# A layer norm moved in between the last output blocks, with its scale and shift folded into the next input

## The chip, the core and the metric

One core of a Trainium2 chip runs the whole program in one launch. The metric is the time of one execution in microseconds on the device, as the median of several runs. The engines are PE (matrix products, with PEld loading its stationary operand), DVE (vector), ACT (activation functions), POOL (GpSimd) and SP, which only issues DMAs here. PSUM is the memory that PE writes, SBUF the one that all engines work in, DRAM what lies behind the DMAs.

## The reference

Four layers on `x` of 512 tokens by 1024 channels, in float32: two of a block that runs an HGRN2 and an RWKV7 mixer side by side, then one RG-LRU and one retention layer with RMS norms. What matters here is how a layer of the first block begins and ends:

```
cond = silu(c) @ w_ada[l] + b_ada[l]
shift, scale, gate_raw = split(cond, 3)
h = x * (1.0 + scale) + shift
proj = h @ w_in[l]
...
out = merged @ w_out[l]
x = layer_norm(DN_ALPHA * x + (1.0 + gate_raw) * out, ln_g[l], ln_b[l])
```

`layer_norm` takes the mean and the variance over the 1024 channels of a token, multiplies by rsqrt(var + 1e-5), then by `g`, and adds `b`. After layer 1 the RG-LRU layer begins with `rms_norm(x, pre0)`, whose sum of squares runs over the same channels.

## The kernel before

Activations are held transposed: channels on the 128 partitions, the 512 tokens along the free axis, so that `x` is eight tiles `xa[:, m, :]` of 128x512. All weights pass through one stream of blocks of eight 128x128 tiles. SP loads block b into one of two buffers `w_raw` (L559), ACT rounds it into `w_hi` (`weights(b)`, L778), POOL writes the rest into `w_lo` (`low`, L702). Activations are split in the same way: ACT writes `act_hi` (`high`, L786), DVE `act_lo` (`low`, L1253). A product is three matmuls, hi·hi, hi·lo and lo·hi; `project` (L1910) does one block of 24 into one of two PSUM banks, `side_by_side` (L1930) four output tiles at once into four banks, taking the input tiles one after the other.

All five engines run programs of their own, in the written order, and meet at counting semaphores. `weights(b)` waits until PE has used block b-2, and SP loads a block when POOL has done with the one two before it. Every engine's order is fixed by hand; there is no planner.

A layer ends so. `side_by_side` makes output tiles 0 to 3, four blocks `b_out+4` to `b_out+7` make tiles 4 to 7. For each tile DVE adds gate times output onto `xa` (`out_added`, L1256). PE sums the channels with a product by a matrix of ones, in plain float32, which is two records in the trace for each tile (`add_up`, L2308): tiles 0 to 3 behind block `b_out+4`, then each tile behind the block after its own. Then, in this order: DVE subtracts the mean from eight tiles; ACT squares each into one of two buffers `ST` (L793) and PE sums the squares (L1952), by turns; ACT makes rsqrt as Ln and Exp (L798, L800), each behind a load of its function table; DVE multiplies each tile by it (L1253) and applies `ln_g`, `ln_b` (L1698), by turns over the eight tiles.

The next layer begins with `modulated` (L1331): DVE writes `x * (1 + scale) + shift` into `ST`, ACT and DVE split it, and PE starts `side_by_side(("rw", l))` on the first tile. ACT's order there is `high` for tiles 0 to 3, `weights(b_rw+2)`, `high` for 4 and 5, `weights(b_rw+3)`, `high` for 6 and 7, `weights(b_rw+4)`, `weights(b_rw+5)`. `x` itself is needed again at the end of the layer, and SP stores it in DRAM:

```
blocks_to(b_rw + 4)
if l:
    sp.wait_ge(S("x_done"), KT * l)
    sp.dma_start(x_scr[0].rearrange("k p t -> p k t"), xa[:, :, :]).then_inc(S("x_saved"), 16)
    blocks_to(b_rw + 6)
    sp.wait_ge(S("x_saved"), 16)
```

`blocks_to(n)` issues the loads of all blocks below n, so the load of block `b_rw+4` stands behind the wait for eight `x_done`. After layer 1 the RMS norm squares `xa` in the same way and PE sums the squares before the first product of the RG-LRU layer. `Chain.done` makes an engine wait for its own instruction.

Of the kernel before, what the change touches and what calls it, by code (L numbers as in the profile page):

```python
# [15 lines left out]
ALU = mybir.AluOpType  # L16
# [4 lines left out]
D = 1024  # L21
# [174 lines left out]
def job_plan():  # L196
    jobs = Jobs()
    for l in range(DEPTH):
# [102 lines left out]
            jobs.add(("out", l, i), i, signalled=False)  # L301
        jobs.add(("ln_mean", l), 4)
        jobs.add(("ln_var", l), 5)
    jobs.add("rms_pre0", 4)
    for i in range(4):
        jobs.add(("lru_in", 0, i), i, signalled=False)
# [47 lines left out]
def build(nc, shapes):  # L354
# [10 lines left out]
    with ExitStack() as ctx:  # L365
# [32 lines left out]
        for name, n in [("c", 8), ("lb_t", 12), ("cl", RT), ("cl_t", RT)] + [  # L398
                (f"{k}{l}", n) for l in range(DEPTH)
                for k, n in (("mu1", 17), ("omlb", 4), ("lbf", 4), ("ka1", 4))]:  # L400
            derived_at[name] = derived[:, used:used + n]
            derived_first[name] = used
            used += n
# [55 lines left out]
        def evacuated(eng, b):  # L459

            u = use_of(b)
            eng.wait_ge(proj_read[u % 2], u // 2 + 2)

        def job_open(eng, name, turn=0):

            bank, use = jobs(name, turn)
            wait(eng, aux_read[bank], use)
            return aux[bank][:, :]

        def job_full(ins, name):  # L470
            return ins.then_inc(aux_full[jobs(name)[0]], 1)
# [295 lines left out]
        def _(act):  # L767
# [20 lines left out]
            def square(key, m, src):  # L788


                if m > 1:
                    act.wait_ge(sq_used, SQUARES[key] - list(SQUARES).index(key) + m - 1)
                A(ST[m % 2], src, ACT.Square).then_inc(sq_ready, 1)  # L793
# [286 lines left out]


            def squares(key, tiles, which, ready):
# [165 lines left out]
        def _(dve):  # L1248
# [3 lines left out]
            def tt(out_ap, a, b, op):  # L1252
                return TT(out_ap, a, b, op)  # L1253
# [60 lines left out]
            def conditioned(l, half, spans):  # L1314

                x = job_ready(dve, ("ada", l, half))
                for at, n in spans:
                    ins = tt(cond[:, l, at:at + n], x[:, at:at + n], V(f"b_ada{l}", at, n), ALU.add)
                    job_read(ins, ("ada", l, half)) if at == spans[-1][0] else ins
                evacuated_job(dve, ("ada", l, half))  # L1320
                for at, n in spans[1:]:
                    chain.done(TS(cond[:, l, at:at + n], cond[:, l, at:at + n], 1.0, None, ALU.add))

            def modulated(l, m):

# [35 lines left out]
            for l in range(DEPTH):  # L1361
# [2 lines left out]

                if l == 0:
                    conditioned(0, 1, ((4, 4), (12, 4)))
                tiles_of_h = range(KT) if l else range(4, KT)
                for m in tiles_of_h:
                    modulated(l, m)
                    if m > tiles_of_h[0]:  # L1370
                        low(SPLITS["h", l] + m - 1, m - 1, ST[(m - 1) % 2])
                low(SPLITS["h", l] + 7, 7, ST[1])
                if l == 0:
                    for n in range(LATER_AT[1]):
                        later_step(n)

# [59 lines left out]
                        .then_inc(S("rk_ready"), 1)  # L1436
                if l == 0:
                    conditioned(1, 0, ((0, 8), (8, 16)))
                for j in range(QT):
                    x = job_ready(dve, ("kk_sum", l, j))  # L1440
                    job_read(TS(xa[:, 4 + j, :], x, 1e-24, None, ALU.max), ("kk_sum", l, j))
# [237 lines left out]
                    else:  # L1679
                        read(ins, b_out + m)  # L1680

                for m in range(KT):
                    out_added(m)
                x = job_ready(dve, ("ln_mean", l))
                for m in range(KT):
                    if m < 4:
                        evacuated_job(dve, ("out", l, m))
                    else:
                        evacuated(dve, b_out + m)
                    ins = stt(xa[:, m, :], x, -1.0 / D, xa[:, m, :], ALU.mult, ALU.add)  # L1690
                    job_read(ins, ("ln_mean", l)) if m == 7 else ins.then_inc(S("xc_ready"), 1)
                dve.wait_ge(S("ln_rs"), l + 1)
                for m in range(KT + 1):
                    if m < KT:
                        tt(xa[:, m, :], xa[:, m, :], merged[:, 0, :], ALU.mult).then_inc(S("ln_scaled"), 1)
                    if m:
                        dve.wait_ge(S("ln_scaled"), KT * l + m)
                        TS(xa[:, m - 1, :], xa[:, m - 1, :], V(f"ln_g{l}", m - 1), V(f"ln_b{l}", m - 1),  # L1698
                           ALU.mult, ALU.add).then_inc(S("x_done"), 1)
                dve.wait_ge(S("x_done"), KT * (l + 1))  # L1700

            def normed(n, pre, count):

# [186 lines left out]
        def _(pe):  # L1890
# [44 lines left out]
            def used(ins):  # L1935

                ins.then_inc(block_used, 1)
# [18 lines left out]
            for l in range(DEPTH):  # L1956
# [344 lines left out]
                x = job_open(pe, ("ln_mean", l))  # L2301

                def add_up(m):
                    if m < 4:
                        evacuated_job(pe, ("out", l, m))
                    else:
                        evacuated(pe, b_out + m)
                    return MM(x, C("ones"), xa[:, m, :], start=(m == 0), stop=(m == 7))  # L2308

                for m in range(4, KT):  # L2310
                    used(project(b_out + m, tiles=(4, 5, 6, 7, 0, 1, 2, 3)))
                    for k in (range(4) if m == 4 else (m - 1,)):
                        add_up(k)
                job_full(add_up(7), ("ln_mean", l))
                sum_squares(("ln", l), ("ln_var", l))


            sum_squares("pre0", "rms_pre0")
# [181 lines left out]
```

## Time and profile before

| | |
|---|---|
| median of 3 runs | 2173.45 us (2170.6 to 2173.84) |
| profiled execution | 2173.69 us |
| its span | 2171.9 us |
| PE busy in the span | 1917.3 us (88%) |
| DVE, ACT, POOL busy | 1011.8, 865.7, 601.4 us |
| mean granted clock of PE | 0.956 |

Times in the profile count from the start of its span. A row of the timeline has the start, the length and, in brackets, how long the engine had been idle before it and what released it; "x8" behind it merges eight instructions. A PE matmul overlaps its neighbours, so that its pace is the distance of starts and not its length. A granted clock of 1.00 is 2.4 GHz, 0.50 is 1.2 GHz.

### The profile page before, as it was taken

The numbers are of one execution on the slowest core, as the hardware profiler recorded it, in microseconds if no ns is written. First come the engines' busy times: TensorE is split into PE (matmuls) and PEld (weight loads), VectorE is DVE, ScalarE is ACT, GpSimd is POOL, SyncE is SP. The second block draws the span as 40 slices with busy tenths as digits, with TensorE's granted clock in tenths as the row PEclk, the third lists the DMA queues.
The fourth block names the chain that finished last, engine by engine and source line by source line (L and its number), as shares of the span: only waits on it lengthen the run. The fifth ranks groups of instructions, "written<-read, shape, count | busy, mean of one in ns | idle before, by whom it ended". The sixth has DMA issues, their size and how long they took to land.

```text
span 2171.9 us, 35369 instructions
## 1 busy us (share of the span) xinstructions
PE 1917.3 (88%) x14368; PEld 1530.4 (70%) x14368; DVE 1011.8 (47%) x1327; ACT 865.7 (40%) x1236; POOL 601.4 (28%) x255
## 2 busy tenths in 40 slices
PE   4999988899997996988899998799687999998987
PEld 3777877699775684877798765666565886777755
DVE  7576376632535046375632635847605224132232
ACT  2333455533523333456433524256524332233332
POOL 1343432300242343422300331321232441322312
PEclk9899999999998898999999998899899999999999
DMA  8662222200423121222200423211133221211111
GB/s 325 215 223 68 80 90 82 68 4 4 171 91 111 62 95 58 88 82 72 69 4 18 170 87 145 78 59 39 43 117 112 97 97 39 78 55 62 59 66 71
DMA packets 60826, 192.89 MB, mean 89 GB/s; under 512 B 5632, under 2 KB 5888, under 8 KB 60320
## 3 DMA queue, kind: packets, MB, share of 16 engines
q1 hardware_dynamic: 60704, 191.10, 25.5%
q8 instruction: 97, 1.59, 0.3%
q14 instruction: 25, 0.20, 0.0%
HBM read 173.25 MB, written 17.83 MB: 88 GB/s over the span
## 4 chain that ended last, share of the span: by engine, by line
issue 57%; PE 24%; POOL 11%; DVE 4%; ACT 3%; POOLq 0%; DVEq 0%; ACTq 0%
PE proj L1910 13%; POOL w_lo_sb L702 10%; PE aux L2120 3%; PE aux L2051 2%; DVE area_sb L1253 2%; PE aux L2177 1%; PE proj L2120 1%; PE aux L2174 1%; ACT L798 1%; DVE area_sb L1256 0%; ACT L905 0%; PE aux L2107 0%; PE aux L1952 0%; PE aux L1941 0%; PE aux L2029 0%
## 5 line engine op out<-in xcount | busy, mean ns | idle before, releaser
L702 POOL TENSOR_TENSOR w_lo_sb<-w_raw_sb,w_hi_sb 128x1024 fp32r<-128x1024 f32 x231 | 583.2, 2525 | 1361.6 <-ACT w_hi_sb L778 1361.6
L1910 PE MATMUL proj<-act_hi_sb,w_hi_sb 128*128 128x512 f32 x1480 | 604.6, 409 | 66.2 <-POOL w_lo_sb L702 49.3
L1910 PE MATMUL proj<-act_lo_sb,w_hi_sb 128*128 128x512 f32 x1480 | 584.4, 395 | 0.0
L1910 PE MATMUL proj<-act_hi_sb,w_lo_sb 128*128 128x512 f32 x1480 | 584.3, 395 | 0.0
L778 ACT ACTIVATE w_hi_sb<-w_raw_sb 128x1024 fp32r<-128x1024 f32 x231 | 244.3, 1058 | 737.1 <-PE proj L1910 521.7
L1910 PEld LDWEIGHTS proj<-act_hi_sb,w_hi_sb 128*128 128x128 f32 x1480 | 283.2, 191 | 140.0 <-POOL w_lo_sb L702 46.1
L1910 PEld LDWEIGHTS proj<-act_lo_sb,w_hi_sb 128*128 128x128 f32 x1480 | 283.2, 191 | 62.7 <-issue 6.7
L1910 PEld LDWEIGHTS proj<-act_hi_sb,w_lo_sb 128*128 128x128 f32 x1480 | 282.7, 191 | 60.9
L1930 PE MATMUL aux<-act_hi_sb,w_hi_sb 128*128 128x512 f32 x336 | 139.0, 414 | 57.8 <-issue 43.2
L1253 DVE TENSOR_TENSOR area_sb<-area_sb 128x256 f32<-128x256 f32 (+2 forms) x208 | 141.5, 719 | 19.9 <-ACT area_sb L930 11.8
L1930 PE MATMUL aux<-act_lo_sb,w_hi_sb 128*128 128x512 f32 x336 | 136.2, 405 | 0.0
L1930 PE MATMUL aux<-act_hi_sb,w_lo_sb 128*128 128x512 f32 x336 | 136.0, 405 | 0.0
L1930 PEld LDWEIGHTS aux<-act_hi_sb,w_hi_sb 128*128 128x128 f32 x336 | 66.7, 198 | 76.8 <-issue 49.9
L1253 DVE TENSOR_TENSOR area_sb<-area_sb,slots_sb 128x512 f32<-128x512 f32 (+1 forms) x90 | 74.1, 839 | 47.3 <-ACT slots_sb L800 36.3
L1253 DVE TENSOR_TENSOR slots_sb<-proj,stage_sb 128x512 f32<-128x512 f32 x28 | 19.3, 690 | 159.1 <-ACT stage_sb L1200 135.1
L1253 DVE TENSOR_TENSOR slots_sb<-slots_sb 128x512 f32<-128x512 f32 (+1 forms) x48 | 67.1, 1402 | 52.8 <-ACT slots_sb L890 26.9
L1952 PE MATMUL aux<-stage_sb,const_sb 128*128 128x512 f32 x128 | 66.9, 657 | 22.8 <-ACT stage_sb L793 22.8
L1930 PEld LDWEIGHTS aux<-act_lo_sb,w_hi_sb 128*128 128x128 f32 x336 | 66.4, 198 | 14.9 <-issue 1.0
L1930 PEld LDWEIGHTS aux<-act_hi_sb,w_lo_sb 128*128 128x128 f32 x336 | 66.3, 197 | 14.6
L2051 PE MATMUL aux<-area_sb 128*128 128x128 f32 x448 | 59.9, 279 | 17.3 <-DVE area_sb L1253 17.3
L2051 PEld LDWEIGHTS aux<-area_sb 128*128 128x128 f32 x448 | 56.8, 191 | 24.4 <-DVE area_sb L1253 20.7
L2120 PE MATMUL aux<-area_sb 64*64 64x64 f32 x1792 | 69.9, 222 | 3.0 <-issue 2.1
(255 smaller groups left out, 2565.6 us busy)
## 6 DMA issues: line engine op xcount, KB each, us to landing
w_raw_sb<-wall SPq DMA_DIRECT2D x231, 512.0 KB, 3.2
area_sb<-w_ada SPq DMA_DIRECT2D x32, 512.0 KB, 4.8
slots_sb<-w_ada SPq DMA_DIRECT2D x16, 512.0 KB, 8.3
gate_scr<-stage_sb SPq DMA_DIRECT2D x32, 256.0 KB, 2.2
area_sb<-gate_scr SPq DMA_DIRECT2D x8, 1024.0 KB, 9.5
x_scr<-area_sb SPq DMA_DIRECT2D x3, 2048.0 KB, 7.4
area_sb<-x_scr SPq DMA_DIRECT2D x3, 2048.0 KB, 9.7
area_sb<-lru_gates SPq DMA_DIRECT2D x1, 3584.0 KB, 11.7
```

What stands on the lines that cost most here:

```text
L702: nc.gpsimd.tensor_tensor(w_lo[:, b % 2, :, :].rearrange("p k n -> p (k n)"), w_raw[:, b % 2, :], w_hi[:, b % 2, :, :].rearrange("p k n -> ...
L778: A(w_hi[:, b % 2, :, :].rearrange("p k n -> p (k n)"), w_raw[:, b % 2, :], ACT.Copy)\
L798: job_read(A(dst, x, ACT.Ln, scale=scale, bias=eps), job)
L1253: return TT(out_ap, a, b, op)
L1910: ins = MM(bank, w[:, s, k, :], a[:, t, :], start=(start and i == 0), stop=(stop and i == len(terms) - 1))
L1930: ins = MM(bank, w[:, s, 4 * (k % 2) + i, :], a[:, t, :], start=(k == 0 and n == 0), stop=(k == len(tiles) - 1 and n == 2))
L1952: ins = MM(x, C("ones"), ST[m % 2], start=(m == 0), stop=(m == tiles - 1))
L2051: ins = MM(x[:, cols], r, r, start=True, stop=True)
L2120: ins = MM(x[q, columns * j:columns * j + columns], a[q, j, :], b(q, j), start=(i == 0), stop=(i == len(products) - 1))
L2174: MM(x[q, 64 * j:64 * j + 64], xt[q, j, :], z[q, j, :], start=True, stop=True)
L2177: ins = MM(x[q, at:at + 64], z[q, j, :], xt[q, j, :], start=True, stop=True)
```

## The change

The layer norm no longer waits for all eight tiles before it subtracts. DVE subtracts the mean of tiles 0 to 3 (their sum over 512) from all eight `xa` tiles behind block `b_out+4`, before tiles 5 to 7 have their outputs. Squares are taken of these shifted tiles and summed by PE among the last three blocks, block `b_out+7` being cut in two. A second sum over tiles 4 to 7, `ln_delta`, gives what is left of the mean; ACT squares it over 1024, DVE takes it off the mean square, and DVE subtracts it from all tiles before the multiplication. On ACT `weights(b_out+9)`, the second block of the next layer, moves behind the Exp.

Between layers 0 and 1, `ln_g0`, `ln_b0` and the conditioning are one scale and one shift (`h_scale`, `h_shift`, three small DVE operations in layer 0), so that DVE makes `h` from the normalised tile, and ACT makes `x` from it in place with an Identity behind each `high`, counting `x_done`. After layer 1, ACT squares `g * tile + b` for the RMS norm and DVE makes `x` behind it. SP and POOL have the same programs as before.

```diff
@@ jobs: ("ln_delta", l) on PSUM bank 4 @@
@@ ACT, start of a layer @@
                 for m in range(KT):
                     high(SPLITS["h", l] + m, m, ST[m % 2])
+                    if l:
+                        A(xa[:, m, :], xa[:, m, :], ACT.Identity, scale=V("ln_g0", m), bias=V("ln_b0", m))\
+                            .then_inc(S("x_done"), 1)
                     if m > 2 and m % 2:
                         weights(b_rw + m // 2 + 1)
@@ ACT, end of a layer @@
-                for m in range(3, KT + 2):
+                for m in range(3, 7):
                     weights(b_out + m)
-                for m in range(KT):
-                    if m < 7:
-                        act.wait_ge(S("xc_ready"), 7 * l + m + 1)
-                    else:
-                        evacuated_job(act, ("ln_mean", l))
-                    square(("ln", l), m, xa[:, m, :])
-                inverse_root(merged[:, 0, :], ("ln_var", l), 1.0 / D, 1e-5, S("ln_rs"))
...
+                ln_squares(0, 1)
+                weights(b_out + 7)
+                ln_squares(2, 3, 4, 5)
+                weights(b_out + 8)
+                ln_squares(6, 7)
+                A(merged[:, 1, :], job_ready(act, ("ln_delta", l)), ACT.Square, scale=1.0 / D).then_inc(S("ln_dsq"), 1)
+                evacuated_job(act, ("ln_var", l))
+                chain.done(A(merged[:, 0, :], merged[:, 0, :], ACT.Ln, bias=1e-5))
+                A(merged[:, 0, :], merged[:, 0, :], ACT.Exp, scale=-0.5).then_inc(S("ln_rs"), 1)
+                weights(b_out + 9)
@@ ACT, after layer 1 @@
-            rms("pre0", "rms_pre0", xa, lambda m: act.wait_ge(S("x_done"), KT + m + 1))
+            for m in range(KT):
+                act.wait_ge(S("ln_scaled"), KT + m + 1)
+                square("pre0", m, xa[:, m, :], scale=V("ln_g1", m), bias=V("ln_b1", m))
+            inverse_root(RS, "rms_pre0", 1.0 / D, 1e-6, S("rms_rs"))
@@ DVE, preparation in layer 0, behind conditioned(1, 0, ...) @@
+                    chain.done(tt(DV["h_scale"], V("ln_g0"), cond[:, 1, 8:16], ALU.mult))
+                    chain.done(tt(DV["h_shift"], V("ln_b0"), cond[:, 1, 8:16], ALU.mult))
+                    chain.done(tt(DV["h_shift"], DV["h_shift"], cond[:, 1, 0:8], ALU.add))
@@ DVE, end of a layer @@
-                for m in range(KT):
+                for m in range(5):
                     out_added(m)
                 x = job_ready(dve, ("ln_mean", l))
                 for m in range(KT):
...
+                    ins = stt(xa[:, m, :], x, -1.0 / HALF, xa[:, m, :], ALU.mult, ALU.add)
+                    job_read(ins, ("ln_mean", l)) if m == 7 else ins.then_inc(S("xc_ready"), 1)
+                for m in range(5, KT):
...
+                    out_added(m)
+                x = job_ready(dve, ("ln_var", l))
+                dve.wait_ge(S("ln_dsq"), l + 1)
+                job_read(stt(merged[:, 0, :], x, 1.0 / D, merged[:, 1, :], ALU.mult, ALU.subtract), ("ln_var", l))
+                x = job_ready(dve, ("ln_delta", l))
...
                     ins = stt(xa[:, m, :], x, -1.0 / D, xa[:, m, :], ALU.mult, ALU.add)
...
                 dve.wait_ge(S("ln_rs"), l + 1)
...
+                if l == 0:
+                    for m in range(KT + 2):
+                        if m < KT:
+                            ln_scaled(m)
+                        if 0 < m <= KT:
+                            next_h(m - 1)
+                        if m > 1:
+                            low(SPLITS["h", 1] + m - 2, m - 2, ST[m % 2])
+                else:
+                    for m in range(KT):
+                        ln_scaled(m)
+                    for m in range(KT):
+                        dve.wait_ge(sq_ready, SQUARES["pre0"] + m + 1)
+                        TS(xa[:, m, :], xa[:, m, :], V("ln_g1", m), V("ln_b1", m), ALU.mult, ALU.add)\
+                            .then_inc(S("x_done"), 1)
@@ PE, end of a layer @@
+                used(project(b_out + 4, tiles=outs))
+                mean_of_first()
+                used(project(b_out + 5, tiles=outs))
+                add_sq(0, 1, 2, 3)
+                used(project(b_out + 6, tiles=outs))
+                add_rest(4)
+                add_rest(5)
+                add_sq(4, 5)
+                project(b_out + 7, tiles=outs[0:4], rows=range(0, 4), stop=False)
+                add_rest(6)
+                add_sq(6)
+                used(project(b_out + 7, tiles=outs[4:], rows=range(4, 8), start=False, open_bank=False))
+                add_rest(7)
+                add_sq(7)
```

`ln_scaled(m)` multiplies tile m by the inverse root (both in SBUF), `next_h(m)` writes `tile * h_scale + h_shift` into `ST[m % 2]`, `add_sq(m)` is the sum over `ST[m % 2]` by ones, `add_rest(m)` the sum of tile m into `ln_delta`, each two matmul records.

## Rows read from the trace of the kernel before

**Rows 1.** Parts 1 (busy us) and 6 (issues, KB, us to landing) of the page.
```profile
PE 1917.3 (88%) x14368; PEld 1530.4 (70%) x14368; DVE 1011.8 (47%) x1327; ACT 865.7 (40%) x1236; POOL 601.4 (28%) x255
...
w_raw_sb<-wall SPq DMA_DIRECT2D x231, 512.0 KB, 3.2
```

**Rows 2.** Timeline of PE, end of layer 0: start us, us, engine, line, operation, count, idle before.
```profile
654.22 7.67 PE L1952 MATMUL aux<-stage_sb,const_sb 128*128 128x512 f32 x16 [1.54 <-ACT stage_sb L793]
675.21 0.76 PE L1930 MATMUL aux<-act_hi_sb,w_hi_sb 128*128 128x512 f32 x1 [13.33 <-issue]
```

**Rows 3.** Stages: length, busy us of PE, PEld, DVE, ACT, POOL, granted clock, DMA.
```profile
675.20:680.40 5.20, 5.19 (x12) 4.11 (x13) 3.93 (x7) 1.26 (x2) 0.00 (x0) 0.51 0.90 321
...
1319.90:1324.70 4.80, 0.00 (x0) 0.00 (x0) 2.10 (x3) 3.78 (x6) 0.00 (x0) 0.72 0.47 167
1324.70:1330.00 5.30, 5.19 (x15) 4.12 (x16) 4.82 (x8) 1.26 (x2) 0.00 (x0) 0.61 0.02 5
```

**Rows 4.** Timeline of ACT, end of layer 0.
```profile
650.81 1.06 ACT L778 ACTIVATE w_hi_sb<-w_raw_sb 128x1024 fp32r<-128x1024 f32 x1 [5.27 <-PE proj L1910]
...
660.73 1.28 ACT L798 ACT_TABLE_LOAD   x1
662.02 0.60 ACT L798 ACTIVATE slots_sb<-aux 128x512 f32<-128x512 f32 x1
...
663.93 0.63 ACT L800 ACTIVATE slots_sb<-slots_sb 128x512 f32<-128x512 f32 x1
```

**Rows 5.** Timeline of DVE, end of layer 0.
```profile
650.75 0.75 DVE L1256 SCALAR_TENSOR_TENSOR area_sb<-proj,cond_sb,area_sb 128x512 f32<-128x512 f32 x1 [5.58 <-PE proj L1910]
652.72 4.87 DVE L1256 SCALAR_TENSOR_TENSOR area_sb<-aux,area_sb 128x512 f32<-128x512 f32 x8 [1.22 <-PE aux L2308]
664.59 1.29 DVE L1253 TENSOR_TENSOR area_sb<-area_sb,slots_sb 128x512 f32<-128x512 f32 x2 [7.00 <-ACT slots_sb L800]
665.80 0.54 DVE L1698 TENSOR_SCALAR area_sb<-area_sb,vec_sb 128x512 f32<-128x512 f32 x1
...
674.42 0.69 DVE L1253 TENSOR_TENSOR act_lo_sb<-stage_sb,act_hi_sb 128x512 fp32r<-128x512 f32 x1 [0.24 <-ACT act_hi_sb L786]
```

**Rows 6.** Timelines of POOL and of DVE where they meet.
```profile
651.94 2.35 POOL L702 TENSOR_TENSOR w_lo_sb<-w_raw_sb,w_hi_sb 128x1024 fp32r<-128x1024 f32 x1 [3.93 <-ACT w_hi_sb L778]
684.57 2.41 POOL L702 TENSOR_TENSOR w_lo_sb<-w_raw_sb,w_hi_sb 128x1024 fp32r<-128x1024 f32 x1 [30.27 <-ACT w_hi_sb L778]
...
685.04 2.48 DVE L1253 TENSOR_TENSOR act_lo_sb<-stage_sb,act_hi_sb 128x512 fp32r<-128x512 f32 x1 [5.80 <-ACT act_hi_sb L786]
```

**Rows 7.** Timeline of SP's DMA issues, start of layer 1.
```profile
673.17 0.38 SPq L634 DMA_DIRECT2D x_scr<-area_sb  x1
687.00 5.77 SPq L559 DMA_DIRECT2D w_raw_sb<-wall  x2
...
694.48 0.42 SPq L642 DMA_DIRECT2D area_sb<-v_scr  x1
698.02 60.85 SPq L559 DMA_DIRECT2D w_raw_sb<-wall  x9
```

**Rows 8.** DMA issues around 673.2, 694.5 and 698.0 us: KB each, us to landing.
```profile
x_scr<-area_sb SPq DMA_DIRECT2D x1, 2048.0 KB, 7.3
...
area_sb<-v_scr SPq DMA_DIRECT2D x1, 1024.0 KB, 7.5
...
w_raw_sb<-wall SPq DMA_DIRECT2D x1, 512.0 KB, 5.2
```

**Rows 9.** Timeline of ACT, weight splits of layer 1.
```profile
694.31 1.06 ACT L778 ACTIVATE w_hi_sb<-w_raw_sb 128x1024 fp32r<-128x1024 f32 x1 [3.34 <-PE aux L1930]
699.75 1.06 ACT L778 ACTIVATE w_hi_sb<-w_raw_sb 128x1024 fp32r<-128x1024 f32 x1 [4.38 <-PE aux L1930]
```

**Rows 10.** Timeline of ACT, end of layer 1.
```profile
1308.67 0.63 ACT L793 ACTIVATE stage_sb<-area_sb 128x512 f32<-128x512 f32 x1 [1.82 <-DVE area_sb L1698]
```

**Rows 11.** Timeline of DVE, preparation in layer 0.
```profile
188.92 0.69 DVE L1441 TENSOR_SCALAR area_sb<-aux 128x512 f32<-128x512 f32 x1 [0.33 <-PE aux L2023]
```

More of the change, by code:

```diff
@@ L303, in job_plan @@
         jobs.add(("ln_var", l), 5)
+        jobs.add(("ln_delta", l), 4)
     jobs.add("rms_pre0", 4)
@@ L397, in build @@
         derived_at, derived_first, used = {}, {}, 0
-        for name, n in [("c", 8), ("lb_t", 12), ("cl", RT), ("cl_t", RT)] + [
+        for name, n in [("c", 8), ("lb_t", 12), ("cl", RT), ("cl_t", RT), ("h_scale", KT), ("h_shift", KT)] + [
                 (f"{k}{l}", n) for l in range(DEPTH)
@@ L786, in high, with square @@
                 A(act_hi[:, slot, :], src, ACT.Copy).then_inc(split_hi, 1)
-            def square(key, m, src):
+            def square(key, m, src, scale=1.0, bias=0.0):
                 if m > 1:
                     act.wait_ge(sq_used, SQUARES[key] - list(SQUARES).index(key) + m - 1)
-                A(ST[m % 2], src, ACT.Square).then_inc(sq_ready, 1)
+                A(ST[m % 2], src, ACT.Square, scale=scale, bias=bias).then_inc(sq_ready, 1)
             def inverse_root(dst, job, scale, eps, signal, turn=0):
@@ L1070, in _, with ln_squares @@
                 high_merged(7)
-                for m in range(3, KT + 2):
+                for m in range(3, 7):
                     weights(b_out + m)
-                for m in range(KT):
-                    if m < 7:
-                        act.wait_ge(S("xc_ready"), 7 * l + m + 1)
-                    else:
-                        evacuated_job(act, ("ln_mean", l))
-                    square(("ln", l), m, xa[:, m, :])
-                inverse_root(merged[:, 0, :], ("ln_var", l), 1.0 / D, 1e-5, S("ln_rs"))
+                def ln_squares(*which):
+                    for m in which:
+                        if m < 5:
+                            act.wait_ge(S("xc_ready"), 7 * l + m + 1)
+                        else:
+                            evacuated(act, b_out + m)
+                        square(("ln", l), m, xa[:, m, :])
+                ln_squares(0, 1)
[8 more added lines that the diff above has]
+                weights(b_out + 9)
             def squares(key, tiles, which, ready):
@@ L1366, in _ @@
                     conditioned(0, 1, ((4, 4), (12, 4)))
[L1367 to L1372, printed above, removed]
-                if l == 0:
+                if l == 0:
+                    for m in range(4, KT):
+                        modulated(0, m)
+                        if m > 4:
+                            low(SPLITS["h", 0] + m - 1, m - 1, ST[(m - 1) % 2])
+                    low(SPLITS["h", 0] + 7, 7, ST[1])
                     for n in range(LATER_AT[1]):
@@ L1687, in _ @@
                         evacuated_job(dve, ("out", l, m))
-                    else:
+                    elif m == 4:
+                        evacuated(dve, b_out + m)
+                    ins = stt(xa[:, m, :], x, -1.0 / HALF, xa[:, m, :], ALU.mult, ALU.add)
+                    job_read(ins, ("ln_mean", l)) if m == 7 else ins.then_inc(S("xc_ready"), 1)
+                for m in range(5, KT):
+                    if m < 7:
+                        dve.wait_ge(S("xc_ready"), 7 * l + m + 1)
+                    else:
+                        evacuated_job(dve, ("ln_mean", l))
+                    out_added(m)
@@ L1692, in _ @@
                 dve.wait_ge(S("ln_rs"), l + 1)
[L1693 to L1699, printed above, removed]
@@ L1700, in _, with ln_scaled, next_h @@
-                dve.wait_ge(S("x_done"), KT * (l + 1))
+                def ln_scaled(m):
+                    if m < 7:
+                        dve.wait_ge(S("ln_centred"), 7 * l + m + 1)
+                    else:
+                        evacuated_job(dve, ("ln_delta", l))
+                    tt(xa[:, m, :], xa[:, m, :], merged[:, 0, :], ALU.mult).then_inc(S("ln_scaled"), 1)
+                def next_h(m):
+                    if m > 1:
+                        dve.wait_ge(split_lo, SPLITS["h", 1] + m - 1)
+                    dve.wait_ge(S("ln_scaled"), m + 1)
+                    TS(ST[m % 2], xa[:, m, :], DV["h_scale"][:, m:m + 1], DV["h_shift"][:, m:m + 1], ALU.mult, ALU.add)\
+                        .then_inc(split_src, 1)
@@ new lines, in _ @@
+                if l == 0:
[4 more added lines that the diff above has]
+                            next_h(m - 1)
+                        if m > 1:
+                            low(SPLITS["h", 1] + m - 2, m - 2, ST[m % 2])
+                else:
+                    for m in range(KT):
+                        ln_scaled(m)
+                    for m in range(KT):
+                        dve.wait_ge(sq_ready, SQUARES["pre0"] + m + 1)
+                        TS(xa[:, m, :], xa[:, m, :], V("ln_g1", m), V("ln_b1", m), ALU.mult, ALU.add)\
+                            .then_inc(S("x_done"), 1)
+                    dve.wait_ge(S("x_done"), KT * 2)
@@ L2300, in _, with mean_of_first, add_rest, add_sq @@
                     evacuated_job(pe, ("rwb", l, 1, i))
-                x = job_open(pe, ("ln_mean", l))
-                def add_up(m):
-                    if m < 4:
+                outs = (4, 5, 6, 7, 0, 1, 2, 3)
+                def mean_of_first():
+                    x = job_open(pe, ("ln_mean", l))
+                    for m in range(4):
                         evacuated_job(pe, ("out", l, m))
+                        ins = MM(x, C("ones"), xa[:, m, :], start=(m == 0), stop=(m == 3))
+                    job_full(ins, ("ln_mean", l))
+                def add_rest(m):
+                    x = aux[jobs(("ln_delta", l))[0]][:, :] if m > 4 else job_open(pe, ("ln_delta", l))
+                    if m == 4:
+                        pe.wait_ge(S("xc_ready"), 7 * l + 5)
                     else:
                         evacuated(pe, b_out + m)
[L2308 to L2315, printed above, removed]
+                    ins = MM(x, C("ones"), xa[:, m, :], start=(m == 4), stop=(m == 7))
+                    if m == 7:
+                        job_full(ins, ("ln_delta", l))
+                def add_sq(*which):
+                    for m in which:
+                        add_square(("ln", l), ("ln_var", l), m)
+                used(project(b_out + 4, tiles=outs))
[12 more added lines that the diff above has]
+                add_sq(7)
             sum_squares("pre0", "rms_pre0")
```

3 lines of the change are left out of this document (2 added, 1 removed).

## The prediction

> **What bounds the kernel now.** I read part 1 of the page first: PE is busy 1917 of 2171.9 us and no other engine is near it [rows 1]. So time goes where PE stands still or runs slowly, and an edit elsewhere counts only through that. The timeline of PE at the end of layer 0 shows where the change works: 1.54 us of idling before the squares are summed, 16 records of sums, then 13.33 us with nothing until the first product of layer 1 at 675.21 [rows 2]. The stages show what follows such a rest: PE runs the first 5.20 us at a granted clock of 0.51. After the later rest of about 5 us (1319.9 to 1324.8, behind layer 1) 0.61 is granted over 5.30 us [rows 3]. The reader is to see three parts in the rest: the wait for the variance, the inverse root on ACT [rows 4], and DVE's work up to the first tile of `h` [rows 5]. The end of layer 1 repeats it 642.3 us later: the first normalised tile with its scale and shift is ready at 665.80 + 0.54 = 666.34 in layer 0, and the square that waits for it in layer 1 starts at 1308.67 [rows 5, 10].
>
> **Up to the inverse root: nearly nothing.** PE loses no work. From one weight split to the next, a block with one sum takes 5.27 + 1.06 = 6.33 us [rows 4], a block alone 699.75 - 694.31 = 5.44 [rows 9], so a sum is 0.87 with its hand-over. Before, six sums lie ahead of the end of `b_out+7` and ten behind it; now 14 lie ahead and two behind. I take 0.86 x 8 = 6.9, and 0.3 for one wait: `weights(b_out+7)` (1.0 us on ACT) stands ahead of the square of tile 2, which PE then awaits after two sums. DVE's last `out_added` moves from 650.75 [rows 5] to 657.9, with 0.75 us to 658.65. Then PE sums tile 7 (to 659.6) and its square (to 660.6); ACT's square of tile 7 and that of `ln_delta` fit beside them. DVE takes delta squared off at 660.7; the result costs 0.75 and the next instruction can start 0.6 later. ACT's table load ends about 661.75, as it now follows the square of `ln_delta`; Ln starts at 661.8 instead of 662.02, Exp at 663.7 instead of 663.93 [rows 4]. Ten sums' worth of overlap gives 0.2 us at the inverse root: eight sums were moved ahead of the block's end, not removed, and a centring and a subtraction were added.
>
> **Behind it, layer 0.** DVE subtracts delta from eight tiles, 4.87 us as the same shape did before [rows 5], from 661.3 to 666.1. That is 1.8 us past the Exp's end (664.3), so Ln and Exp are hidden and the second centring is on the path. Next comes a wait that the code doesn't show. `weights(b_out+9)` now follows the Exp: ACT 664.3 to 665.35, POOL 665.4 to 667.8. POOL's split and a DVE operation with both inputs in SBUF don't run together: with POOL busy 684.57 to 686.98, the DVE split that began at 685.04 took 2.48 us instead of 0.69, ending 0.54 after POOL. The centring, whose one input is PSUM, ran beside POOL's 651.94 to 654.29 at its usual pace [rows 5, 6]. So the centring passes, and the first multiplication (0.68) begins at 666.0 and ends at 667.8 + 0.54 = 668.35. From there multiplication 1, `next_h(0)`, multiplication 2, `next_h(1)`, `low(0)` take 0.61, 0.46, 0.61, 0.46 and 0.69 [rows 5], with gaps of 0.05: PE starts at 671.2 instead of 675.21. **Gain 4.0 us.** Its bounds: 2.5, if ACT's new steps come one us later and DVE meets more of POOL, and 5.6 with no lock.
>
> The Trainium skill, "SBUF — State Buffer", says that DVE and GpSimd share a port pair as an exclusive lock and that whichever starts first has it for its whole instruction. The trace agrees (2.48 us against 0.69). Without that rule the sum would be 1.6 us better in either layer.
>
> **The store of x, layer 1's start.** This step isn't in the diff, and I hold it for the dearest. SP issues the store of `x` (2 MB) when `x_done` is 8, and the load of block `b_rw+4` stands behind that wait. Before, the store went at 673.17, ahead of PE's start, and the load at 687.00, when its buffer came free [rows 7]. Now `x_done` is counted by ACT, behind each `high`, and ACT's program has `weights(b_rw+2)` and `weights(b_rw+3)` between tiles. `weights(b_rw+3)` came one block before 694.31, at 688.87 [rows 9], which is 13.66 after PE's start; now 671.2 + 13.7 = 684.9, as all that PE does from its start is the same. Behind it `high(6)`, Identity, `high(7)`, Identity follow from 685.85 at 0.6 each: `x_done` is 8 at 688.2. The store is issued there, the load at 688.6. The store took 7.3 us to land [rows 8], thus 695.5. How long the load behind it takes, the nearest row tells: issued at 698.02 behind a 1 MB read that landed at 694.48 + 7.5 = 702.0, it landed at 703.2, 1.2 us later [rows 7, 8]. Here 1.2 to 1.5 behind 695.5 is 697. ACT's part 1.06, POOL's 2.4 and hand-overs: `w_lo` of `b_rw+4` is ready at 700.7. PE needs it when block `b_rw+3` is done, 699.75 - 675.21 = 24.5 after its start [rows 2, 9], at 695.7. **Loss 5.0 us**; bounds 0 (if the load lands 3.2 us after its issue, the median of all such loads [rows 1]) and 7 (3.2 more behind the store). Block `b_rw+5` was issued right behind and is hidden by `b_rw+4`.
>
> PE then has stood 5 us, after which the stage of about the same rest gave 0.61 over 5.30 us: 0.39 x 5.30 = 2.07 us of lost full-speed time [rows 3]. **Loss 2.0**; bounds 0 (the clock holds) and 2.6 (0.49 x 5.20, as at 675.2). Layer 0's end in all: -4.0 + 5.0 + 2.0 = +3.0.
>
> The Trainium skill, "DMA: Bandwidth & Descriptors", section "Queues, rings and completion order", says that one issuing engine has one ring on each DMA engine, consumed in ring order. By this the load cannot pass the store; if transfers shared the bandwidth in packets instead, it could land earlier. The 5.2 us of the row above agree, for a read behind a read; a load behind a write no row shows.
>
> **End of layer 1.** The same times plus 642.3. The first tile for the RMS square was ready at 1308.64; now multiplication 0 ends at 668.35 + 642.3 = 1310.65, since here too `weights(b_out+9)` puts POOL in DVE's way. ACT's square takes scale and bias for nothing, and PE sums the squares at PE's and ACT's pace, as before; the saved turns between multiplication and scaling lie off that path. The scaling of `x` for SP's second store ends later than before, but still with the sums, ahead of PE's start; the load behind it is due some 12 us after that start (687.00 against 675.21 in layer 0 [rows 2, 7]), so nothing slips. **Loss 2.0**; bounds -0.5 (no lock, and a clock that rises one step earlier) and +3.5. The longer rest ahead of these sums (8.7 us) I cost at nothing, because they already ran slowly at first.
>
> **The rest.** Three small DVE operations in layer 0, about 0.6 us, stand ahead of a chain that waits for PE anyway (0.33 at 188.92, and again one tile later) [rows 11]: 0, at most 0.4. Within the three blocks no weight is late: `weights(b_out+8)` is issued when `b_out+6` ends, as before.
>
> **Sum.** On the profiled execution's 2173.69 (span 2171.9): +3.0 + 2.0 = +5.0, 2178.7. The median of the runs is 0.24 lower; I say 2178.5. Within 0.2%, 4.35 us, no difference can be told; the forecast lies just beyond.
>
> **Rivals.**
> A, not slower: the load of `b_rw+4` isn't held up by the store. It lands by 692 and POOL is done at 695.6, just in time; the point is a landing by 692.1, against my 697. For it: the engines may overlap a write to DRAM with a read; the row I use is a read behind a read. Against it: 5.2 us there. The 5.0 and the clock's 2.0 go: -4.0 + 2.0 = -2.0, 2171.5.
> B: the store costs as forecast but POOL isn't met, if Ln and Exp come later or DVE gets in first. PE starts at 669.6, and the load slips as much as PE does: -5.6 + 7.0 in layer 0, and 2.0 - 1.6 = +0.4 in layer 1, together +1.8, 2175.3.
> C, faster: neither happens, -5.6 + 0.4 = -5.2, 2168.3. It needs both, and the meeting with POOL rests on a margin of 0.6 us only.
> D, worse: the load lands 3.2 behind the store (+2) and the slow clock is longer after each rest (+1.5): 2182.
>
> **How the numbers follow.** Forecast 0.60 (its own range 2175.8 to 2181.5), A 0.14, B 0.12, C 0.07, D 0.07. The range runs from A to D: 2171.3 to 2182. Slower by over 0.2% is above 2177.8: some 0.62 of the forecast's 0.60, D and a little of B: 0.46. Faster by over 0.2%, below 2169.1: C and a little of A: 0.08. The rest, 0.46, is no difference.
>
> **What would show it.** In the profile after: PE's first product of layer 1 about 4 us after the end of the Exp's weight split, at 671; a DVE multiplication at 666 of over 2 us beside POOL; the store of x issued at 688 instead of 673, right ahead of a w_raw load that lands over 7 us after its issue; and a PE idle of about 5 us before block `b_rw+4` whose releaser is `w_lo`, followed by slow clock. In layer 1 the first RMS square at 1310.6 plus what layer 0 lost. It would be wrong if PE ran through `b_rw+4`, if the inverse root came over 2 us sooner than 0.2, or if the sums within the blocks made PE wait more than once for ACT.

## The result, and the profile after

The changed kernel took 2175.89 us at the median of 16 runs (2172.28 to 2180.81), the kernel before 2171.91 in runs beside them (2169.7 to 2174.07): ratio 1.0022, 95% interval 1.0014 to 1.0029. By the medians it is slower by 4.0 us, by the ratio by 0.22% or 4.8 us, where the sum of the forecast was +5.0. The profiled execution is the longest of the 16 (2180.81, span 2178.9), so its rows show each mechanism and not the middle of its size.

The timeline of PE after: the first product of layer 1, the product behind block `b_rw+3`, and the first sum of RMS squares behind layer 1.

```profile
671.10 0.76 PE L1989 MATMUL aux<-act_hi_sb,w_hi_sb 128*128 128x512 f32 x1 [10.39 <-issue]
...
703.23 0.80 PE L1969 MATMUL proj<-act_hi_sb,w_hi_sb 128*128 128x512 f32 x1 [7.27 <-POOL w_lo_sb L703]
...
1317.60 1.19 PE L2011 MATMUL aux<-stage_sb,const_sb 128*128 128x512 f32 x1 [8.57 <-ACT stage_sb L794]
```

The first answers to [rows 2]: 671.10 instead of 675.21. The second had no counterpart; PE stood 7.27 us and waited for `w_lo`. The waits of PE from 670 to 760 us name it as one wait:

```profile
PE aux L1989 <- issue: 10.4, 1, 10.4
PE proj L1969 <- POOL w_lo_sb L703: 7.3, 1, 7.3
PE aux L2056 <- ACT slots_sb L854: 1.6, 1, 1.6
```

DVE and POOL behind the norm, which answer to [rows 5, 6]: eight centrings of delta, then two multiplications in 2.75 us where two took 1.29, because POOL's split had begun 0.75 us earlier.

```profile
661.35 4.86 DVE L1275 SCALAR_TENSOR_TENSOR area_sb<-aux,area_sb 128x512 f32<-128x512 f32 x8
666.14 2.75 DVE L1272 TENSOR_TENSOR area_sb<-area_sb,slots_sb 128x512 f32<-128x512 f32 x2
668.81 0.53 DVE L1741 TENSOR_SCALAR stage_sb<-area_sb,derived_sb 128x512 f32<-128x512 f32 x1
```

```profile
665.39 2.34 POOL L703 TENSOR_TENSOR w_lo_sb<-w_raw_sb,w_hi_sb 128x1024 fp32r<-128x1024 f32 x1 [14.64 <-ACT w_hi_sb L779]
```

ACT and SP, for [rows 4, 7 and 9]: the Exp at 663.74 (before 663.93), its last Identity at 687.90, the store right behind it, and the split of `b_rw+4` after 11.00 us of idling, released by its load.

```profile
663.74 0.63 ACT L1094 ACTIVATE slots_sb<-slots_sb 128x512 f32<-128x512 f32 x1
...
687.90 0.80 ACT L817 ACTIVATE area_sb<-area_sb,vec_sb 128x512 f32<-128x512 f32 x1
699.70 1.06 ACT L779 ACTIVATE w_hi_sb<-w_raw_sb 128x1024 fp32r<-128x1024 f32 x1 [11.00 <-DMA w_raw_sb<-wall]
```

```profile
688.72 0.38 SPq L635 DMA_DIRECT2D x_scr<-area_sb  x1
689.16 1.80 SPq L560 DMA_DIRECT2D w_raw_sb<-wall  x2
696.95 0.33 SPq L639 DMA_DIRECT2D area_sb<-up  x1
```

The DMA issues from 688 to 692 us, KB each and median us to landing, for [rows 8]: the two loads took 10.8 us (`b_rw+4` alone 10.5, when ACT begins on it at 699.70), the store 8.2.

```profile
x_scr<-area_sb SPq DMA_DIRECT2D x1, 2048.0 KB, 8.2
w_raw_sb<-wall SPq DMA_DIRECT2D x2, 512.0 KB, 10.8
```

The stages after the two restarts of PE and at the first sums behind layer 1, columns as in [rows 3]; 0.50 is 1.2 GHz:

```profile
671.10:677.10 6.00, 6.00 (x14) 4.74 (x15) 5.94 (x11) 3.51 (x6) 0.00 (x0) 0.50 0.00 0
...
703.20:707.80 4.60, 4.57 (x11) 3.61 (x12) 2.23 (x4) 1.34 (x2) 2.32 (x1) 0.50 0.63 199
1317.60:1322.20 4.60, 4.60 (x6) 1.78 (x6) 4.59 (x9) 2.12 (x3) 0.00 (x0) 0.50 0.24 95
```

The account of the two profiled executions: PE reaches layer 1 4.1 us sooner; it stands 7.3 us before `b_rw+4`; after the first restart it is slow for 6.0 us instead of 5.2, after the second for 4.6, together 0.4 + 2.3 us. These steps add up to +5.9. What became of them later is seen from the start of the same weight split of ACT in both traces:

| weight split | before | after | difference |
|---|---|---|---|
| `b_out+5`, ahead of the changed end of layer 0 | 623.82 | 623.72 | -0.1 |
| `b_rw+11` | 732.39 | 738.39 | +6.0 |
| `b_rw+12` | 754.82 | 755.87 | +1.1 |
| the last before 1230 us | 1228.65 | 1231.80 | +3.2 |
| the next one | 1233.47 | 1239.44 | +6.0 |
| end of the span | 2171.9 | 2178.9 | +7.0 |

So 5 us of the loss came back within one block, in a stretch whose program the change leaves alone. PE was busy for the same 20.38 us of it, but the granted clock was 0.69 before and 0.92 after, and it did 69 matmuls where it had done 50. The stretch from 735 to 757 us, before and then after:

```profile
735.00:757.00 22.00, 20.38 (x50) 11.60 (x50) 0.52 (x1) 9.46 (x15) 1.92 (x2) 0.69 0.07 24
735.00:757.00 22.00, 20.38 (x69) 12.34 (x68) 1.12 (x2) 11.48 (x17) 3.84 (x2) 0.92 0.14 48
```

The same amount was then lost again up to 1240 us, again where nothing was changed. The largest piece, 2.8 us, lies from 1225 to 1240 us, before and then after:

```profile
1225.00:1240.00 15.00, 12.36 (x54) 10.24 (x55) 10.91 (x13) 8.12 (x9) 7.39 (x3) 1.00 0.31 102
1225.00:1240.00 15.00, 12.19 (x42) 9.49 (x41) 8.25 (x11) 6.69 (x6) 4.73 (x2) 0.77 0.21 70
```

At the end of layer 1 the difference is +6.0, by chance the sum of the steps. There the first RMS square starts at 1316.64 against 1308.67 [rows 10], 2.0 more. The spans differ by 7.0; the remaining -0.9 arose behind it and isn't explained further.

### The profile page after: what moved, and what is told of

The parts are those of the page before. It is cut to its first block, busy times and chain, and to the rows that moved or that the text cites. A ratio compares the mean times of both kernels' runs of the same rounds, so it can differ in the third digit from the quotient of the medians.

```text
span 2178.9 us, 35408 instructions
## 1 busy us (share of the span) xinstructions
PE 1916.7 (88%) x14368; PEld 1532.5 (70%) x14368; DVE 1021.4 (47%) x1340; ACT 873.1 (40%) x1246; POOL 601.0 (28%) x255
## 4 chain that ended last, share of the span: by engine, by line
issue 57%; PE 24%; POOL 11%; DVE 4%; ACT 3%; POOLq 0%; DVEq 0%; ACTq 0%
PE proj L1969 13%; POOL w_lo_sb L703 11%; PE aux L2179 3%; PE aux L2110 2%; DVE area_sb L1272 2%; PE aux L2236 1%; PE proj L2179 1%; PE aux L2233 1%; ACT L799 1%; DVE area_sb L1275 0%; ACT L909 0%; PE aux L2166 0%; PE aux L2011 0%; PE aux L2000 0%; PE aux L2088 0%
## 6 DMA issues: line engine op xcount, KB each, us to landing
area_sb<-lru_gates SPq DMA_DIRECT2D x1, 3584.0 KB, 11.6
```

## The experiments

All ratios are to the kernel before, run on the same chip beside them, with 95% intervals. The first four experiments share one chip and its runs of the kernel before, the next four a second, the last has a third.

**The changed kernel again.**

> The changed kernel once more, as the measure for the runs beside it. Theory (order): the load of block b_rw+4 waits behind the 2 MB store of x, PE stands about 5 to 7 us before that block and then runs slowly for 3 to 5 us; POOL's split of b_out+9 holds the first multiplication by 1.6 us at the end of both layers. Total 3 to 5 us over the kernel before. Rival (a lucky pairing of the first profile): the idle of 7.3 us before b_rw+4 is not seen again and the total is within 2 us of the kernel before.

Ratio 1.0025 (1.0015 to 1.0035). In its profile PE idled 10.39 us ahead of layer 1, 7.33 before `b_rw+4` and 8.57 ahead of the RMS sums: the first profile's figures within 0.1. The store's landing isn't chance. The total is 5.4 us over the kernel before by the ratio and 6.7 by the medians, a little more than was expected.

**The loads first.**

```diff
                 blocks_to(b_rw + 4)
                 if l:
+                    blocks_to(b_rw + 6)
                     sp.wait_ge(S("x_done"), KT * l)
```

> The changed kernel, with SP issuing the loads of b_rw+4 and b_rw+5 ahead of its wait for x_done. Theory (order): the load is issued at about 683 and landed by 687, PE runs through b_rw+4, and the idle of 7.3 us and the slow clock behind it (2.3 us) go; what is left is -4.0 in layer 0 and +2.0 at the end of layer 1, so about 2 us under the kernel before and 5 to 9 under the changed one. Rival (the stall has another cause, as ACT being late with its splits for the added Identities): PE still stands over 3 us before b_rw+4 and the total stays 3 to 5 us over the kernel before.

Ratio 1.0025 (1.0013 to 1.0036): no gain, and the theory's time was missed by 7 us. The stall before `b_rw+4` was gone, but PE stood two blocks further on, before `b_rw+6`. PE and SP of this run:

```profile
707.78 0.80 PE L1970 MATMUL proj<-act_hi_sb,w_hi_sb 128*128 128x512 f32 x1 [5.87 <-POOL w_lo_sb L704]
```

```profile
684.20 0.43 SPq L636 DMA_DIRECT2D x_scr<-area_sb  x1
694.39 0.34 SPq L640 DMA_DIRECT2D area_sb<-up  x1
694.77 0.43 SPq L642 DMA_DIRECT2D area_sb<-v_up  x1
695.25 0.42 SPq L644 DMA_DIRECT2D area_sb<-v_scr  x1
696.02 15.20 SPq L560 DMA_DIRECT2D w_raw_sb<-wall  x4
```

POOL had freed the buffer for `b_rw+6` at 689.2. SP could not issue its load, because it stood in the wait for the store to land. The waits of SP from 660 to 720 us show 9.4 us of it:

```profile
SPq L640 <- DMA x_scr<-area_sb: 9.4, 1, 9.4
```

After it came `up`, `v_up` and the 1 MB of `v`, and only then the load at 696.02, whose block ACT could begin 8.2 us later. So the cause was right as to the first place and incomplete: the late store holds SP as well as the ring.

**The order alone.**

```diff
                     sp.wait_ge(S("x_done"), KT * l)
+                    blocks_to(b_rw + 6)
                     sp.dma_start(x_scr[0]...)
```

> The changed kernel, with SP waiting for x_done as before but then issuing the two loads ahead of the store: the same time of issue (about 688.7), the order alone turned. Theory (order in the ring): the load lands 3.2 to 3.5 us after its issue, w_lo is ready at about 695.7, when PE wants it, so PE idles under 1 us; the total is 1 to 2.5 us under the kernel before. Rival (shared bandwidth: a load beside a 2 MB store is slow whichever is first): the load still takes over 7 us, PE still idles 4 us or more, and the total stays 2 us or more over the kernel before.

Ratio 1.0005 (0.9996 to 1.0014). The loads went at 686.79 and the store at 687.66; ACT began on `b_rw+4` at 690.30, so its block took at most 3.5 us to land with the store right behind it, against 10.6 in the run of the changed kernel beside it. That is the order theory's number and not the rival's. The store paid: 11.6 us to land. (The 4.5 below is the median of the two loads.)

```profile
686.79 0.82 SPq L560 DMA_DIRECT2D w_raw_sb<-wall  x2
687.66 0.43 SPq L636 DMA_DIRECT2D x_scr<-area_sb  x1
```

```profile
690.30 1.06 ACT L780 ACTIVATE w_hi_sb<-w_raw_sb 128x1024 fp32r<-128x1024 f32 x1 [3.54 <-DMA w_raw_sb<-wall]
```

```profile
x_scr<-area_sb SPq DMA_DIRECT2D x1, 2048.0 KB, 11.6
w_raw_sb<-wall SPq DMA_DIRECT2D x2, 512.0 KB, 4.5
```

The total was missed, for the reason seen with the loads first: PE stood 6.58 us before `b_rw+6`.

**The split early.**

```diff
-                ln_squares(6, 7)
+                ln_squares(6)
+                weights(b_out + 9)
+                ln_squares(7)
...
-                weights(b_out + 9)
```

> The changed kernel, with ACT's weights(b_out+9) ahead of the square of tile 7 instead of behind the Exp, so that POOL's split runs at about 659 to 661.4. Theory (POOL in DVE's way): the first multiplication takes 0.68 us instead of over 2, PE's first product of layer 1 starts 1.6 us earlier, and so does the first RMS square of layer 1; the stall before b_rw+4 stays. About 3.2 us less than the changed kernel, 0 to +2 against the kernel before. Rival (ACT's 1.0 us ahead of the square of tile 7 is on the path): what the multiplication gains is lost at the Ln, and the total moves under 1 us.

Ratio 1.0007 (0.9998 to 1.0016), 0.18% or 3.9 us under the changed kernel beside it, with intervals that touch. PE's idle time fell from 10.39 to 8.93 us ahead of layer 1 and from 8.57 to 7.10 ahead of the RMS sums, 1.5 each, while the stall before `b_rw+4` stayed at 7.30:

```profile
665.13 0.77 PE L1990 MATMUL aux<-act_hi_sb,w_hi_sb 128*128 128x512 f32 x1 [8.93 <-issue]
...
697.35 0.79 PE L1970 MATMUL proj<-act_hi_sb,w_hi_sb 128*128 128x512 f32 x1 [7.30 <-POOL w_lo_sb L703]
...
1308.62 1.19 PE L2012 MATMUL aux<-stage_sb,const_sb 128*128 128x512 f32 x1 [7.10 <-ACT stage_sb L794]
```

The first two multiplications behind the norm took 1.28 us again, instead of 2.75:

```profile
661.63 1.28 DVE L1273 TENSOR_TENSOR area_sb<-area_sb,slots_sb 128x512 f32<-128x512 f32 x2
```

**The late store alone, in the kernel before.**

```diff
                     sp.wait_ge(S("x_done"), KT * l)
+                    sp.wait_ge(split_hi, SPLITS["h", 1] + 8)
                     sp.dma_start(x_scr[0]...)
```

> The kernel before, with one wait more on SP: the store of x is held until high(7) of layer 1, about 15.7 us after PE's start instead of 2 us before it. Nothing else of the change is in it. Theory (the late store alone makes the stall): the store goes at about 691, the load of b_rw+4 lands about 11 us behind it as in the profile of the changed kernel, w_lo is ready 3.6 us later, at 705.5 against a need at 699.7, so PE idles 5 to 6 us before b_rw+4 and 1.5 to 2.5 us go to the clock: 6 to 8.5 us over the kernel before. Rival (the stall needs the added Identities on ACT or the changed order of DVE): PE idles under 1 us there and the time is that of the kernel before.

Ratio 1.0038 (1.0024 to 1.0051), 6.8 us by the medians (five runs). One wait on SP makes the kernel before at least as slow as the changed one, with no Identity on ACT. PE's idle time was 4.45 us, a little under what was expected, as the load of `b_rw+4` landed 9.1 us after its issue (10.0 is the median of the two):

```profile
703.34 0.50 PE L1911 MATMUL proj<-act_hi_sb,w_hi_sb 128*128 128x512 f32 x1 [4.45 <-POOL w_lo_sb L703]
```

```profile
690.28 0.38 SPq L635 DMA_DIRECT2D x_scr<-area_sb  x1
690.72 1.80 SPq L559 DMA_DIRECT2D w_raw_sb<-wall  x2
```

Its profiled execution is only 3.0 us longer than the profiled one of the kernel before: here too 5.0 us came back between the splits of `b_rw+11` and `b_rw+12`. How the 6.8 us of the medians divide between the stall and the clock, one profile doesn't tell.

**The loads in between.**

```diff
                 if l:
+                    blocks_to(b_rw + 6)
                     sp.wait_ge(S("x_done"), KT * l)
                     sp.dma_start(x_scr[0]...)
-                    blocks_to(b_rw + 6)
+                    blocks_to(b_rw + 7)
                     sp.wait_ge(S("x_saved"), 16)
...
                     sp.dma_start(xa[0:32, 2, :], dram["v_up"]).then_inc(S("up_in"), 16)
+                    blocks_to(b_rw + 8)
                     sp.wait_ge(S("v_out"), 16)
```

> The changed kernel, with the loads of b_rw+4 and b_rw+5 ahead of the wait for x_done (as in the run that issued the loads first), and now also the load of b_rw+6 ahead of SP's wait for the store's landing, and the load of b_rw+7 ahead of the 1 MB read of v. Theory (in that run the stall moved two blocks on, because SP stood 9.4 us waiting for the store and the load of b_rw+6 came behind the read of v): PE has no idle time over 1 us in the first 60 us of layer 1; the total is -4.0 in layer 0 and +2.0 at the end of layer 1, about 2 us under the kernel before and 5 to 7 under the changed one. Rival (the DMA engines lack the bandwidth for the store and the stream together, whatever the order): PE still idles 3 us or more somewhere among b_rw+4 to b_rw+9, and the total is no better than with the loads first.

Ratio 0.9987 (0.9976 to 0.9999), 2.2 us under the kernel before by the medians. All the waits of PE from 672 to 760 us, behind the one ahead of layer 1, are now these:

```profile
PE aux L1991 <- issue: 10.4, 1, 10.4
PE aux L2058 <- ACT slots_sb L856: 1.6, 1, 1.6
```

So the bandwidth is there; the order was the fault. What remains are the two terms that the forecast had without the store, -4.0 and +2.0, and the time agrees with their sum.

**Both.** This edit and the early split together:

```diff
                 ln_squares(6)
+                weights(b_out + 9)
                 ln_squares(7)
...
+                    blocks_to(b_rw + 6)
                     sp.wait_ge(S("x_done"), KT * l)
```

> The same, with weights(b_out+9) ahead of the square of tile 7 as well. Theory: both effects are independent, so 1.5 us less at each of the two ends of a layer: about 5 us under the kernel before. Rival (the slow clock's length is set by where its steps fall and swallows such gains): under 2 us between this and the run without the early split.

Ratio 0.9989 (0.9977 to 1.0002). The idle times fell as before (8.93 and 7.11 us), and the profiled span was 2164.3 against 2170.5; but the medians, 2169.35 and 2169.48, don't show it. Of the 6.2 us between the two spans, 2.8 had arisen ahead of the changed code (the split of `b_out+5` begins at 623.26 against 626.05). The spread of these runs (2159.96 to 2173.5) is larger than the 3 us in question. The expected 5 us under the kernel before were not reached, and the comparison of the times is undecided.

**The second centring cut.** This is added to both edits. `centred(m)` is the second centring of tile m, cut out of its loop over eight tiles; layer 1's multiplications have the same two lines.

```diff
-                for m in range(KT):
...
+                for m in range(5):
+                    centred(m)
...
                         if m < KT:
                             ln_scaled(m)
+                        if 2 < m < 6:
+                            centred(m + 2)
```

> The same again, with DVE's second centring cut: tiles 0 to 4 before the wait for the inverse root, tiles 5 to 7 each behind a multiplication (3, 4 and 5). Theory (the second centring is on the path because it ends 1.8 us behind the Exp): PE's first product of layer 1 and the first RMS square of layer 1 come 1.7 us earlier, and the total is 3 to 4 us under the run before this one, about 8.5 under the kernel before. Rival (ACT's and DVE's turns on the first tiles pace PE anyway): PE starts no earlier than in the run with the early split, and the total stays within 1 us of it.

Ratio 0.9983 (0.9973 to 0.9993). Ahead of layer 1 PE idled 7.20 us instead of 8.93, as expected. The total is 3.7 us under the kernel before, not the expected 8.5. Ahead of the RMS sums PE idled 9.24 instead of 7.11, which the expectation didn't have, and here the releaser is DVE and no longer ACT:

```profile
1304.04 1.22 PE L2022 MATMUL aux<-stage_sb,const_sb 128*128 128x512 f32 x1 [9.24 <-DVE area_sb L1278]
```

```profile
1298.49 2.50 DVE L1275 TENSOR_TENSOR area_sb<-area_sb,slots_sb 128x512 f32<-128x512 f32 x4
...
1303.31 0.68 DVE L1278 SCALAR_TENSOR_TENSOR area_sb<-aux,area_sb 128x512 f32<-128x512 f32 x1
```

```profile
1299.22 1.52 ACT L796 ACTIVATE stage_sb<-area_sb,vec_sb 128x512 f32<-128x512 f32 x2 [0.76 <-DVE area_sb L1275]
1306.22 0.81 ACT L796 ACTIVATE stage_sb<-area_sb,vec_sb 128x512 f32<-128x512 f32 x1 [5.48 <-PE aux L2022]
```

The first two squares were ready at 1300.7. PE started 0.05 us after the centring of tile 7, the last reader of `ln_delta` in PSUM bank 4, and the plan gives `rms_pre0` the same bank.

**Another bank.**

```diff
-    jobs.add("rms_pre0", 4)
+    jobs.add("rms_pre0", 5)
```

> The interleaved kernel, with the sum of squares of the RMS norm (rms_pre0) on PSUM bank 5 instead of bank 4, which it shared with ln_delta. Theory (in the interleaved run PE waited 9.24 us before that sum, released by DVE's centring of tile 7, which was the last to read ln_delta's bank and now comes 4 us later): PE's first sum of RMS squares follows the first square by 0.2 us, the wait falls from 9.2 to about 5.3 us, and the total comes 3 to 4 us under the interleaved run, about 7.5 us under the kernel before, ratio 0.9965. Rival (PE waits there for the squares, not for the bank): the wait stays near 9 us and the time is that of the interleaved run.

Ratio 0.9968 (0.9958 to 0.9979), 2166.32 us against 2172.76: 6.4 us under the kernel before. It has the lowest ratio of all versions, though its interval overlaps those of the three before it. The wait became 5.38 us and is ended by ACT's square again:

```profile
1297.83 1.19 PE L2022 MATMUL aux<-stage_sb,const_sb 128*128 128x512 f32 x1 [5.38 <-ACT stage_sb L796]
```

## Why the prediction was right

**Up to the inverse root** the forecast stands: 0.2 us gained, Exp at 663.74 against 663.7. (Two slips in the working don't matter: by its own rows a sum is 6.33 - 5.44 = 0.89 us and not 0.87, and eight sums were moved, not ten.) The last `out_added` came at 657.92 against 657.9, and delta squared was taken off at 660.75 against 660.7.

**Layer 0 behind it**: PE at 671.10 against 671.2. That the second centring is on the path, and that POOL's split holds the multiplication, are two separate terms, and they were taken away one after the other (the early split 1.5 us, then the cut centring 1.7). The Trainium skill's rule of the exclusive lock ("SBUF — State Buffer", section "Who interferes with whom") agrees with 2.75 us for two multiplications and with their 1.28 once the split is early.

**The store**: place, releaser and order as forecast; the store went at 688.72 against 688.2. The term that was mis-sized is the landing of the load behind it: 697 was reckoned, 699.7 measured, so that the idle time is 7.3 us and not 5.0. The load was issued 0.5 us later than reckoned, the store took 8.2 us instead of 7.3, and the load landed 2.7 us behind the store instead of 1.2 to 1.5. The row that the last figure came from is one load issued 3.5 us into a 1 MB read; here two loads stood right behind 2 MB. From 695.97 to 703.2 us the DMA engines were busy 0.95 of the time. The kernel before with the store held back shows that a late store alone makes such a stall. It is 4.45 us there, because the store went 16.0 us behind PE's start and not 17.6, and the load landed 9.1 us after its issue and not 10.5.

The Trainium skill ("DMA: Bandwidth & Descriptors", section "Queues, rings and completion order") says that each DMA engine takes an issuing engine's descriptors in ring order, but that a later one may finish its write before an earlier one. The prediction's "cannot pass" says more than that. The trace agrees with the order: the load landed 3.5 us after its issue ahead of the store, and 10.6 us after it behind the store.

**The clock** cost 2.3 us after the stall, 2.0 reckoned, and 0.4 more after the first restart, which was costed at nothing. What the forecast did not have at all is that the clock differs later on too: it gave 5 us back between 735 and 757 us and took about as much again by 1240. From the split of `b_rw+11` to that of `b_rw+12` there are 17.4 to 17.5 us in both profiles of the changed kernel, with the order swapped, with the early split and in the kernel before with the late store. There are 22.2 to 22.5 in the kernel before, with the loads first and in all later versions. PE's idle time in the stretch is the same 1.6 us in all, so the difference is the clock's. What decides it isn't shown; a stall ahead of it doesn't by itself, as the version with the loads first had one of 5.87 us.

**Layer 1**: 2.0 us, as forecast; that ACT's squares cost more with scale and bias (below) didn't show, as PE's slow sums set the pace. **The three small operations** cost nothing: they ran from 186.10 to 186.67, and the four operations behind them ran without a gap, where two had waited for PE before [rows 11]. DVE in layer 0 after:

```profile
186.10 0.37 DVE L1272 TENSOR_TENSOR derived_sb<-vec_sb,cond_sb 128x8 f32<-128x8 f32 x2
186.50 0.17 DVE L1272 TENSOR_TENSOR derived_sb<-derived_sb,cond_sb 128x8 f32<-128x8 f32 x1
186.70 2.48 DVE L1462 TENSOR_SCALAR area_sb<-aux 128x512 f32<-128x512 f32 x4
```

The sum was +5.0; the profile shows +7.0, the medians +4.0 and the ratio +4.8. The mechanism was right, but that the size comes out so close is partly luck. Up to 738 us the forecast had +3.0 and the profile shows +6.0, and what the clock then gave and took, which the forecast did not have, is as large as the whole effect. The 2175.89 us lie just inside the forecast's own range from 2175.8, and that with a kernel before that ran 1.5 us faster beside it than in the runs that the sum started from. Rival A fell with the load's 10.5 us, B and C with the 2.75 us. What the forecast didn't see is the second trap behind the first, SP's wait for the store's landing. It costs nothing in the changed kernel, where `b_rw+4` is late anyway, and comes forward as soon as that is mended.

Open is why executions of one kernel spread so far: 7.7 us over 35 runs of the kernel before and 10.6 over 27 on another chip, 8.5 over 16 of the changed one, 13.5 over the run with both edits. The idle times before each restart repeat within 0.1 us from profile to profile, the stretches of slow clock behind them don't (6.0 and 4.9 us after the first restart in the two profiles of the changed kernel). A part of the spread is there before the changed end of layer 0 begins: the split of `b_out+5` starts anywhere from 619.24 to 626.05 us in the eleven profiles, though only three small operations ahead of it differ. So 1 or 2 us less idle time need not show in the medians, and here mostly didn't.

## What to carry to other kernels

When a result is produced later by an engine off the path, look at what waits for it in another engine's program order: here a store that had been early became the one thing ahead of a weight load, and a wait for its landing held the next ones. Issue what the path needs ahead of a bulk transfer, and put bulk transfers right behind a load, where they have a whole block's time. When work moves across a stage's border, check the shared resources that it is moved past: POOL's turn at SBUF cost 1.5 us of idling at each end of a layer here, and the PSUM bank of the next sum 3.9 us in the version with the centring cut. And read what a stall costs at the end of the program and not only where it stands: on this kernel a later stretch gave back 5 of 6 us, and others took them again.

## What was not expected of the hardware

Two 512 KB loads right behind a 2 MB store landed 10.0 to 10.9 us after their issue (medians of the pair), the first of them after 9.1 to 10.6, where the median of all weight loads is 3.2 [rows 1]. Issued 0.9 us ahead of the store the first took at most 3.5, and the store then 11.6 instead of 7.3 [rows 8]. An Identity with a scale and a bias from SBUF took 0.80 us where the plain rounding beside it took 0.61 to 0.63, and the squares likewise 0.81 for 0.63. The forecast had given the scale and the bias for nothing. The Trainium skill ("ScalarE: Activation LUTs", section "What ACT_TABLE_LOAD costs") says that each such operand adds about 93 ns, and two of them agree with the 0.18 us.
